# TensorE's two waits for a near down block, moved in front of the up tile that precedes the block

## The chip, the core and the metric

The kernel runs on one core of one Trainium2 chip. The metric is the device time of one execution in microseconds (us), the median of several runs. All numbers of matrices are float32; most products are made from split operands (below).

## What is computed

A block of a network for 256 tokens with 1024 features: six feed-forwards, and between them a mixer, a recurrent layer and an attention layer. The six feed-forwards are most of the work, and the only part that the change touches:

```python
def swiglu_ffn(x, w_in, w_out):                    # D_MODEL = 1024, D_FF = 2816
    gate, up = jnp.split(x @ w_in, 2, axis=-1)
    return (jax.nn.silu(gate) * up) @ w_out

x = x + 0.5 * swiglu_ffn(rms_norm(x, g), w_in, w_out)    # six times, other layers between
```

## The kernel before

**Tiles.** The hidden features of a feed-forward are cut into 22 parts (NFC) of 128, numbered c. For each part there is a *gate* tile and an *up* tile: eight steps over the 1024 input features, accumulated in one bank of PSUM. Then there is the *near* block of the part, which multiplies hid(c) by the part's rows of w_out for the first half of the outputs (four output tiles, accumulated over all c in banks 0 to 3). The second half of the outputs comes at the end, in twelve *far* blocks. Gate and up tiles use banks 4 to 7, in turn.

**Split products.** A float32 weight block w arrives by DMA in `raw`, ACT (ScalarE) rounds it into `w_hi` (L666), and POOL (GpSimd, L571) or DVE (VectorE, L1105) makes the rest `w_lo` = raw - w_hi. `three_products` makes two matmuls of a pair of weight tiles: w_hi on both halves of the moving operand (512 columns, L1866) and w_lo on the high half (256 columns, L1867). So a gate or up tile is 16 matmuls, a near block 8.

**The ring.** Weight blocks go through six slots in a written order. A slot's semaphores are `arrived`, `hi_ready`, `lo_ready` and `used`; TensorE raises `used` with the last matmul of a block, ACT waits for it before it writes the slot's w_hi again, and the load of a further block waits for `lo_ready`.

**The hidden part.** When the up tile of c is done, ACT copies the low halves out of PSUM (`take_low`, L783), DVE adds them (L1211, raises `halves_added`), multiplies by rstd (L1221), ACT takes the silu (L788), and DVE makes hid(c) in three operations (L1230, L1231, L1232; the last raises `h_ready`). Between these DVE makes the low parts of some weight blocks. Its order is written out by hand in `hidden(c)`: the low part of near block c - 1 comes first in `hidden(c)` for c > 1, so behind hid(c - 1); that of near block 0 comes inside `hidden(0)`. A near block's low part is the 128x512 form of L1105.

**TensorE's order.** In `ffn`: the tiles of c = 0 and 1, then gate_up(2), then 19 times `down(k)` and `gate_up(k + 3)` (LEAD = 3, FFN_STEPS = 19), then the near blocks 19, 20, the first far block, near block 21 and the other far blocks. `down(c)` waits for `h_ready` of c and for the `lo_ready` of its weight block. A gate tile waits for `halves_added` of part c - 2, which frees its banks, and for its `lo_ready`; an up tile waits for its `lo_ready` alone. The phases are ffn_a to ffn_f. In ffn_c DVE has also a gained copy of x to make (`gain_x`) from c = 3 on.

**Waits on TensorE.** Where an instruction has one wait, it is part of the weight load. Where it has more, the profile shows an EVENT_SEMAPHORE instruction on TensorE's sequencer with the rest of them (L1880, L1936).

Of the kernel before, what the change touches and what calls it, by code (L numbers as in the profile page):

```python
# [18 lines left out]
NFC = FF // P  # L19
# [20 lines left out]
LEAD = 3  # L40
UNUSED_PRODUCTS = 9
FFN_STEPS = NFC - LEAD
# [8 lines left out]
def gate_block(c):  # L51

    return 2 * c if c < LEAD else 2 * LEAD + 1 + 3 * (c - LEAD)


def stored_down(c):

    return 2 * LEAD + 3 * c if c < FFN_STEPS else 2 * LEAD + 3 * FFN_STEPS + c - FFN_STEPS
# [10 lines left out]
def near_block(c):  # L69

    return NEAR_LAST if c == NFC - 1 else stored_down(c)
# [141 lines left out]
def slot(n):  # L213

    return n % RING
# [20 lines left out]
def nth_split(n):  # L236

    return SPLITS_SO_FAR[n]
# [34 lines left out]
def build(nc, x_in, blocks, consts, out):  # L273
    ctx = ExitStack()
    with ctx:
# [3 lines left out]
        def sem(name):  # L279
            return ctx.enter_context(nc.semaphore(name))  # L280
# [48 lines left out]
        lo_ready = [sem(f"lo_ready{s}") for s in range(RING)]  # L329
# [24 lines left out]
        h_ready = sem("h_ready")  # L354
# [1503 lines left out]
        def _(pe):  # L1858
# [5 lines left out]
            def three_products(where, hi, lo, both, opens, closes):  # L1864

                nc.tensor.matmul(where, hi, both.rearrange("p a t -> p (a t)"), start=opens, stop=False)  # L1866
                return nc.tensor.matmul(where[:, 0:SEQ], lo, both[:, 0, :], start=False, stop=closes)  # L1867

            def feature_tiles(tiles, after_norm=None, between=None, in_halves=False):

                for k in range(KD):
                    if after_norm is not None:
                        pe.wait_ge(xn_lo_ready, KD * SPLIT_NORMS.index(after_norm) + k + 1)
                    for n, b in tiles:
                        if k == 0 and in_halves:
                            pe.wait_ge(half_lo, n + 1)
                        elif k == (KD // 2 if in_halves else 0):
                            pe.wait_ge(lo_ready[slot(n)], nth_split(n))  # L1880
                        wh, wl = (w[:, slot(n), k * P:k * P + P] for w in (w_hi, w_lo))
                        ins = three_products(ps[:, b, :], wh, wl, xn[:, k, :, :], k == 0, k == KD - 1)
                        if k == KD - 1:
                            ins.then_inc(used[slot(n)], 1)
                    if between and k == between[0]:
                        between[1]()
# [46 lines left out]
            def near_products(n0, c):  # L1933

                n = n0 + near_block(c)
                pe.wait_ge(lo_ready[slot(n)], nth_split(n))  # L1936
                for d in range(NEAR):
                    wh, wl = (w[:, slot(n), d * P:d * P + P] for w in (w_hi, w_lo))
                    ins = three_products(ps[:, d, :], wh, wl, hid[:, c, :, :], c == 0, c == NFC - 1)
                ins.then_inc(used[slot(n)], 1)  # L1940

            def far_products(n0, i):

                n, pair_no = n0 + far_block(i), i // len(GROUPS)
                group = GROUPS[i % len(GROUPS)]
                pe.wait_ge(lo_ready[slot(n)], nth_split(n))
                for d in range(2):
                    for o, c in enumerate(group):
                        at = o * PAIR + d * P
                        wh, wl = (w[:, slot(n), at:at + P] for w in (w_hi, w_lo))  # L1950
                        ins = three_products(ps[:, (4 if pair_no == 0 else 0) + d, :], wh, wl, hid[:, c, :, :], c == 0, c == NFC - 1)
                    if n == NRING - 1 and d == 0:
                        ins.then_inc(acc_done, 1)
                ins.then_inc(used[slot(n)], 1)
# [46 lines left out]
            def ffn(f, phase, total=total_squares):  # L2001
                n0 = FIRST[phase]

                def bank_of(c):
                    return 4 + 2 * (c % 2)

                def gate_up(c):
                    if c >= 2:
                        pe.wait_ge(halves_added, NFC * f + c - 1)
                    feature_tiles([(n0 + gate_block(c), bank_of(c))])  # L2010
                    feature_tiles([(n0 + gate_block(c) + 1, bank_of(c) + 1)])

                def down(c):
                    pe.wait_ge(h_ready, NFC * f + c + 1)
                    near_products(n0, c)
                norm = ("g_ffn_a", "g_ffn_b", "both", "g_ffn_d", "g_ffn_e", "g_ffn_f")[f]
                if f == 0:

                    feature_tiles([(n0, bank_of(0))], after_norm=norm, in_halves=True)
                    feature_tiles([(n0 + 1, bank_of(0) + 1)], in_halves=True)  # L2020
                    feature_tiles([(n0 + 2, bank_of(1))])
                elif norm == "both":
                    feature_tiles([(n0, bank_of(0)), (n0 + 1, bank_of(0) + 1), (n0 + 2, bank_of(1))], after_norm=norm,
                                  between=(6, total))
                elif norm == "g_ffn_e":
                    for n, b in ((n0, bank_of(0)), (n0 + 1, bank_of(0) + 1), (n0 + 2, bank_of(1))):
                        feature_tiles([(n, b)], after_norm=norm)
                    total()
                else:
                    feature_tiles([(n0, bank_of(0)), (n0 + 1, bank_of(0) + 1), (n0 + 2, bank_of(1))], after_norm=norm)  # L2030
                feature_tiles([(n0 + 3, bank_of(1) + 1)], between=None if norm in ("both", "g_ffn_e") else (1, total))
                gate_up(2)
                for k in range(FFN_STEPS):
                    down(k)
                    gate_up(k + LEAD)
                down(NFC - 3)
                down(NFC - 2)
                far_products(n0, 0)
                down(NFC - 1)
                for i in range(1, N_FAR):  # L2040
                    if i == len(GROUPS):
                        pe.wait_ge(x_ready, 4 * UPDATES_BEFORE[phase] + 1)
                    far_products(n0, i)
                pe.wait_ge(x_ready, 4 * UPDATES_BEFORE[phase] + 3)
# [421 lines left out]
            def attention():  # L2466
# [85 lines left out]
            steps = [  # L2552
                lambda: None,
                lambda: ffn(0, "ffn_a"),
                lambda: (pe.wait_ge(const_loaded, 16), mixer_one()),
                lambda: None,
                lambda: ffn(1, "ffn_b"),
                lambda: None,
                lambda: ffn(2, "ffn_c", lambda: total_squares(2, True)),
                lambda: lru(),  # L2560
                lambda: ffn(3, "ffn_d"),
# [125 lines left out]
```

## Time and profile before

| | us |
|---|---|
| median of 3 runs | 1521.01 (1520.73 to 1521.26) |
| the profiled execution | 1521.21 |
| its span, first to last instruction | 1519.4 |
| PE (TensorE matmul) busy | 1510.9 (99%) |
| DVE busy | 1052.7 (69%) |
| POOL busy | 923.4 (61%) |
| ACT busy | 776.9 (51%) |

The granted clock of TensorE was 1.0 over the span (2.4 GHz). The difference of 1.8 us between the profiled execution and its span lies before the first and behind the last instruction. Matmuls are pipelined: a row's duration is longer than the distance to the next one's start, so distances are read from start to start.

### The profile page before, as it was taken

How to read it: one execution, taken by the hardware profiler on the slowest of the kernel's cores; microseconds unless marked ns; L12 is line 12 of the kernel's file. 1: busy time of each engine (PE TensorE's matmuls, PEld its weight loads, DVE VectorE, ACT ScalarE, POOL GpSimd, SP SyncE). 2: the span in 40 equal slices, each digit the busy share in tenths (PEclk: the TensorE clock that was granted, in tenths of full speed). 3: DMA queues.
4: the chain of work that ended last, by engine and by line, in shares of the span. 5: the costliest groups of instructions: out<-in, count | busy, mean ns of one | idle time of the engine just before them, and what ended most of it. 6: DMA issues, size and time to landing. Idle time of an engine off the chain costs nothing.

```text
span 1519.4 us, 24540 instructions
## 1 busy us (share of the span) xinstructions
PE 1510.9 (99%) x9480; PEld 1315.8 (87%) x9480; DVE 1052.7 (69%) x1472; ACT 776.9 (51%) x1125; POOL 923.4 (61%) x1092
## 2 busy tenths in 40 slices
PE   9999999999999999999999999999999999999998
PEld 7888888888888888888899888888888887888887
DVE  7966555666986668976587986655466666797664
ACT  6554441123655455455567655456555456665542
POOL 4966520201687677876766687578776673168663
PEclk9999999999999999999999999999999999999999
DMA  8665633222565564665634565565555562346553
GB/s 302 209 196 183 205 99 115 85 79 86 199 212 183 168 215 160 192 205 165 228 126 167 186 210 185 183 215 187 162 189 189 186 207 94 138 156 207 188 165 119
DMA packets 113491, 263.64 MB, mean 174 GB/s; under 512 B 9184, under 2 KB 51296, under 8 KB 113248
## 3 DMA queue, kind: packets, MB, share of 16 engines
q1 hardware_dynamic: 113376, 262.09, 52.5%
q8 instruction: 75, 1.23, 0.3%
q14 instruction: 40, 0.33, 0.1%
HBM read 261.00 MB, written 1.05 MB: 172 GB/s over the span
## 4 chain that ended last, share of the span: by engine, by line
PE 74%; DVE 1%; ACT 0%; issue 0%; DVEq 0%; ACTq 0%
PE ps L1866 40%; PE ps L1867 21%; PE ps L1961 2%; PE ps L1982 2%; PE ps L1898 1%; PE ps L1899 1%; PE ps L1897 1%; PE ps L2434 1%; PE ps L2436 1%; PE ps L2435 1%; PE ps L2387 1%; PE ps L1997 0%; PE ps L1998 0%; PE ps L1996 0%; DVE arena L1812 0%; PE ps L1929 0%
## 5 line engine op out<-in xcount | busy, mean ns | idle before, releaser
L571 POOL TENSOR_TENSOR w_lo<-raw,w_hi 128x256 fp32r<-128x256 f32 x1056 | 902.4, 887 | 475.1 <-ACT w_hi L666 471.6
L1866 PE MATMUL ps<-xn,w_hi 128*128 128x512 f32 x2112 | 741.2, 393 | 0.4 <-POOL w_lo L571 0.2
L1867 PE MATMUL ps<-xn,w_lo 128*128 128x256 f32 x2112 | 591.4, 280 | 0.0
L666 ACT ACTIVATE w_hi<-raw 128x1024 fp32r<-128x1024 f32 (+1 forms) x516 | 475.5, 932 | 186.0 <-PE ps L1867 146.1
L1866 PEld LDWEIGHTS ps<-xn,w_hi 128*128 128x128 f32 x2112 | 395.1, 187 | 90.1 <-issue 0.7
L1867 PEld LDWEIGHTS ps<-xn,w_lo 128*128 128x128 f32 x2112 | 398.9, 189 | 0.2
L1866 PE MATMUL ps<-hid,w_hi 128*128 128x512 f32 x1056 | 379.4, 396 | 0.0
L1105 DVE TENSOR_TENSOR w_lo<-raw,w_hi 128x512 fp32r<-128x512 f32 (+1 forms) x245 | 284.8, 1163 | 32.5 <-ACT w_hi L666 27.6
L1867 PE MATMUL ps<-hid,w_lo 128*128 128x256 f32 x1056 | 297.1, 281 | 0.0
L1866 PEld LDWEIGHTS ps<-hid,w_hi 128*128 128x128 f32 x1056 | 198.4, 188 | 49.4
L1211 DVE TENSOR_TENSOR arena<-ps,low_part 128x512 f32<-128x512 f32 x132 | 90.8, 688 | 202.9 <-ACT low_part L783 202.9
L1867 PEld LDWEIGHTS ps<-hid,w_lo 128*128 128x128 f32 x1056 | 198.5, 188 | 0.0
L783 ACT ACTIVATE low_part<-ps 128x512 f32<-128x512 f32 x132 | 78.3, 593 | 163.8 <-PE ps L1867 163.6
L788 ACT ACTIVATE arena<-arena 128x256 f32<-128x256 f32 x132 | 55.3, 419 | 149.4 <-DVE arena L1221 149.4
L1221 DVE TENSOR_TENSOR arena<-arena,rstd 128x512 f32<-128x512 f32 x132 | 113.7, 861 | 4.5
L1913 PE MATMUL ps<-xs,raw 128*128 128x256 f32 x432 | 98.2, 382 | 0.0
L1231 DVE TENSOR_TENSOR h<-arena 128x256 f32<-128x256 f32 x132 | 91.5, 694 | 0.0
L1913 PEld LDWEIGHTS ps<-xs,raw 128*128 128x128 f32 x432 | 80.6, 190 | 12.2 <-issue 1.1
L1232 DVE TENSOR_TENSOR hid<-h,hid 128x256 fp32r<-128x256 f32 x132 | 86.0, 651 | 4.5
L1230 DVE TENSOR_TENSOR hid<-arena 128x256 fp32r<-128x256 f32 x132 | 60.7, 460 | 29.1 <-ACT arena L788 29.1
L1253 DVE SCALAR_TENSOR_TENSOR x<-ps,x 128x512 f32<-128x512 f32 x23 | 15.8, 686 | 59.6 <-PE ps L1867 59.6
L612 POOL TENSOR_TENSOR arena<-arena 128x512 f32<-128x512 f32 x4 | 4.5, 1113 | 77.5 <-DVE arena L1327 77.2
(345 smaller groups left out, 1305.8 us busy)
## 6 DMA issues: line engine op xcount, KB each, us to landing
raw<-blocks SPq DMA_DIRECT2D x418, 512.0 KB, 3.7
raw<-blocks SPq DMA_DIRECT2D x146, 256.0 KB, 3.5
cst<-consts SPq DMA_DIRECT2D x1, 2358.0 KB, 14.5
x<-x_in SPq DMA_DIRECT2D x4, 256.0 KB, 5.9
out<-x SPq DMA_DIRECT2D x4, 256.0 KB, 3.3
cst<-consts SPq DMA_DIRECT2D x1, 109.0 KB, 2.1
```

The lines of the kernel that those rows point to most:

```text
L571: ins = nc.gpsimd.tensor_tensor(w_lo[:, slot(n), piece], raw[:, slot(n), piece], w_hi[:, slot(n), piece], ALU.subtract)
L666: nc.scalar.activation(w_hi[:, slot(n), cols], raw[:, slot(n), cols], ACT.Copy)\
L783: nc.scalar.activation(low_part[:, :, :], ps[:, b:b + 2, SEQ:], ACT.Copy).then_inc(low_taken, 1)
L1105: nc.vector.tensor_tensor(w_lo[:, slot(n), cols], raw[:, slot(n), cols], w_hi[:, slot(n), cols], ALU.subtract).then_inc(lo_ready[slot(n)], 1)
L1211: nc.vector.tensor_tensor(gate_up[:, :, :], ps[:, b:b + 2, 0:SEQ], low_part[:, :, :], ALU.add)\
L1221: nc.vector.tensor_tensor(gate_up[:, :, :], gate_up[:, :, :], over(rstd[:, :], 2), ALU.mult)\
L1230: nc.vector.tensor_tensor(hid[:, c, 0, :], gate_up[:, 1, :], gs, ALU.mult)
L1231: chain(nc.vector.tensor_tensor(h[:, :], gate_up[:, 1, :], gs, ALU.mult))
L1232: nc.vector.tensor_tensor(hid[:, c, 1, :], h[:, :], hid[:, c, 0, :], ALU.subtract)\
L1866: nc.tensor.matmul(where, hi, both.rearrange("p a t -> p (a t)"), start=opens, stop=False)
L1867: return nc.tensor.matmul(where[:, 0:SEQ], lo, both[:, 0, :], start=False, stop=closes)
L1913: ins = nc.tensor.matmul(where, raw[:, slot(n), k * P:k * P + P], xs[:, k, :], start=k == 0, stop=k == KD - 1)
```

## The change

The wait for the weight block goes out of `near_products`. A new function `down_ready(c)` holds both waits of a near block. It is called between the gate tile and the up tile of gate_up(c + 2) for c = 0 to 19, and for c = 20 and 21 in `down(c)`, as before. Nothing else is changed.

```diff
@@ -1933,7 +1933,6 @@
             def near_products(n0, c):
 
                 n = n0 + near_block(c)
-                pe.wait_ge(lo_ready[slot(n)], nth_split(n))
                 for d in range(NEAR):
...
@@ -2004,14 +2003,22 @@
                 def bank_of(c):
                     return 4 + 2 * (c % 2)
 
+                def down_ready(c):
+                    n = n0 + near_block(c)
+                    pe.wait_ge(h_ready, NFC * f + c + 1)
+                    pe.wait_ge(lo_ready[slot(n)], nth_split(n))
+
                 def gate_up(c):
                     if c >= 2:
                         pe.wait_ge(halves_added, NFC * f + c - 1)
                     feature_tiles([(n0 + gate_block(c), bank_of(c))])
+                    if c >= LEAD - 1:
+                        down_ready(c + 1 - LEAD)
                     feature_tiles([(n0 + gate_block(c) + 1, bank_of(c) + 1)])
 
                 def down(c):
-                    pe.wait_ge(h_ready, NFC * f + c + 1)
+                    if c >= FFN_STEPS + 1:
+                        down_ready(c)
                     near_products(n0, c)
```

## Rows read from the trace of the kernel before

**Rows 1.** The page: engines' busy time, and the chain that ended last.

```profile
PE 1510.9 (99%) x9480; PEld 1315.8 (87%) x9480; DVE 1052.7 (69%) x1472; ACT 776.9 (51%) x1125; POOL 923.4 (61%) x1092
...
PE ps L1866 40%; PE ps L1867 21%; PE ps L1961 2%; PE ps L1982 2%; PE ps L1898 1%; PE ps L1899 1%; PE ps L1897 1%; PE ps L2434 1%; PE ps L2436 1%; PE ps L2435 1%; PE ps L2387 1%; PE ps L1997 0%; PE ps L1998 0%; PE ps L1996 0%; DVE arena L1812 0%; PE ps L1929 0%
```

**Rows 2.** Order of time, weight loads in ffn_a: an up tile's, two near blocks' (start, duration).

```profile
59.50 0.19 PEld L1866 LDWEIGHTS ps<-xn,w_hi 128*128 128x128 f32 x1
...
62.28 0.19 PEld L1866 LDWEIGHTS ps<-hid,w_hi 128*128 128x128 f32 x1
...
69.26 0.19 PEld L1866 LDWEIGHTS ps<-hid,w_hi 128*128 128x128 f32 x1
```

**Rows 3.** Order of time, VectorE: low part of the near block of 69.26.

```profile
61.67 1.11 DVE L1105 TENSOR_TENSOR w_lo<-raw,w_hi 128x512 fp32r<-128x512 f32 x1
```

**Rows 4.** Order of time, start of ffn_d: VectorE, then first loads of near blocks 0, 1.

```profile
854.88 0.43 DVE L1232 TENSOR_TENSOR hid<-h,hid 128x256 fp32r<-128x256 f32 x1
856.51 0.69 DVE L1211 TENSOR_TENSOR arena<-ps,low_part 128x512 f32<-128x512 f32 x1 [1.21 <-ACT low_part L783]
...
862.28 1.11 DVE L1105 TENSOR_TENSOR w_lo<-raw,w_hi 128x512 fp32r<-128x512 f32 x1
...
857.49 0.19 PEld L1866 LDWEIGHTS ps<-hid,w_hi 128*128 128x128 f32 x1
...
864.48 0.19 PEld L1866 LDWEIGHTS ps<-hid,w_hi 128*128 128x128 f32 x1
```

**Rows 5.** The same of near block 1 in ffn_a, b, c, e, f; block 3 of ffn_c.

```profile
31.11 1.11 DVE L1105 TENSOR_TENSOR w_lo<-raw,w_hi 128x512 fp32r<-128x512 f32 x1
...
34.33 0.19 PEld L1866 LDWEIGHTS ps<-hid,w_hi 128*128 128x128 f32 x1
...
402.86 1.11 DVE L1105 TENSOR_TENSOR w_lo<-raw,w_hi 128x512 fp32r<-128x512 f32 x1
...
406.16 0.19 PEld L1866 LDWEIGHTS ps<-hid,w_hi 128*128 128x128 f32 x1
...
590.08 1.11 DVE L1105 TENSOR_TENSOR w_lo<-raw,w_hi 128x512 fp32r<-128x512 f32 x1
...
592.30 0.19 PEld L1866 LDWEIGHTS ps<-hid,w_hi 128*128 128x128 f32 x1
...
1087.60 1.11 DVE L1105 TENSOR_TENSOR w_lo<-raw,w_hi 128x512 fp32r<-128x512 f32 x1
...
1095.49 0.19 PEld L1866 LDWEIGHTS ps<-hid,w_hi 128*128 128x128 f32 x1
...
1351.92 1.11 DVE L1105 TENSOR_TENSOR w_lo<-raw,w_hi 128x512 fp32r<-128x512 f32 x1
...
1354.52 0.19 PEld L1866 LDWEIGHTS ps<-hid,w_hi 128*128 128x128 f32 x1
...
603.35 0.72 DVE L1105 TENSOR_TENSOR w_lo<-raw,w_hi 128x512 fp32r<-128x512 f32 x1
...
606.27 0.19 PEld L1866 LDWEIGHTS ps<-hid,w_hi 128*128 128x128 f32 x1
```

**Rows 6.** Order of time, ffn_a: GpSimd's last piece, and the weight load it released.

```profile
20.98 0.73 POOL L571 TENSOR_TENSOR w_lo<-raw,w_hi 128x256 fp32r<-128x256 f32 x1
...
21.82 0.19 PEld L1866 LDWEIGHTS ps<-xn,w_hi 128*128 128x128 f32 x1 [0.52 <-issue]
```

**Rows 7.** Order of time, matmuls: pairs 3, 4 of ffn_d's block 0; pair 3 of ffn_a's block 20.

```profile
858.31 0.42 PE L1866 MATMUL ps<-hid,w_hi 128*128 128x512 f32 x1
...
858.69 0.39 PE L1866 MATMUL ps<-hid,w_hi 128*128 128x512 f32 x1
...
162.35 0.39 PE L1866 MATMUL ps<-hid,w_hi 128*128 128x512 f32 x1
```

**Rows 8.** TensorE's event instructions: before a near block in ffn_a; before gate tiles in ffn_d.

```profile
L1936 PEldq EVENT_SEMAPHORE  x1: 51/51/51, 66.3 to 66.3; - x1
...
L1880 PEldq EVENT_SEMAPHORE  x2: 51/51/51, 858.6 to 863.6; - x2
```

## The prediction, made before the changed kernel was run

> **What bounds the kernel now.** First the page: TensorE (PE) is busy 1510.9 us of the span and its two lines L1866 and L1867 carry the chain that ended last [rows 1]. So only what PE does, or what makes PE wait, can move the end, and any time in which PE stands still is added in full unless PE has idle time further on that swallows it; it has 8.5 us of such time in the whole kernel. The question is therefore where TensorE would arrive at the moved waits before their semaphores are there.
>
> The second view is the order of time inside a feed-forward. In the steady state the up tile starts at 59.50, the near block behind it at 62.28, the next near block at 69.26 [rows 2]: an up tile takes 2.78 us (16 matmuls in pairs of 0.347 us) and one iteration 6.98 us. The moved waits therefore ask for their semaphores 2.78 us earlier than now. Nothing stands still in these iterations: the 114 distances from one near block to the next are all 6.96 to 6.99 us, of which rows 2 show one.
>
> **The change, part by part.** In each of the six feed-forwards, 20 near blocks (c = 0 to 19) lose both waits at their start, and the same two waits come before the up tile of gate_up(c + 2). The blocks 20 and 21 keep theirs where they were. No matmul, weight load, DMA or semaphore is added or taken away: 120 pairs of waits move past 16 matmuls each. Queued behind them on PE are the up tile, the near block and the next gate tile; who waits for these is ACT (low_part of the up tile), DVE behind it, and the ring (ACT's splitting into w_hi and the loads on SP's queue wait for the slots). They are all late by the same amount as PE, no more. No other queue is passed.
>
> *Late iterations: nothing.* Once VectorE has caught up, the last of the two semaphores is the one of the near block's low parts. For the near block at 69.26 it comes at 61.67 + 1.11 = 62.78 [rows 3], and the up tile in front starts at 69.26 - 2.78 = 66.48: 3.7 us to spare, against 6.5 us now, and more later, as VectorE goes on to catch up. The wait costs nothing there; what hides it is VectorE's lead of a whole iteration.
>
> *First iterations: TensorE stands still.* At the start of a feed-forward VectorE has no lead: it has just made rstd. In the fourth one (ffn_d) h(0) is there at 854.88 + 0.43 = 855.31; near block 0 starts at 857.49, in time [rows 4], but its up tile starts at 857.49 - 2.78 = 854.71: 0.60 us late. Worse is the next one. The low half of near block 1 is made by VectorE behind h(1), at 862.28 + 1.11 = 863.39, and near block 1 starts at 864.48; its up tile starts at 864.48 - 2.78 = 861.70, so TensorE would wait 1.69 us [rows 4]. The same subtraction for the others [rows 5], low half of near block 1 against the start of near block 1 less 2.78:
> ffn_a 32.22 - 31.55 = 0.67; ffn_b 403.97 - 403.38 = 0.59; ffn_c 591.19 - 589.52 = 1.67; ffn_f 1353.03 - 1351.74 = 1.29; ffn_e 1088.71 against 1092.71, 4.0 us to spare. Sum with ffn_d: 5.91 us.
>
> The stall at up tile 2 (h(0), 0.60 us in ffn_d, and about as much or less in the other four, where the same steps of VectorE stand in the same place) is not added to that, if what makes block 1 late isn't driven by TensorE: the late moment is then fixed, and the first stall only brings TensorE there later. I take that, since between h(0) and the low half of block 1 VectorE waits only once, 1.21 us for ACT's low_part of tiles finished before [rows 4], and works without a gap otherwise. Behind block 1 the shift of 0.6 to 1.7 us is itself the margin for the following blocks: the tightest is ffn_c, where the gained copy of x holds VectorE up. Its near block 3 is at 606.27 with its low half at 603.35 + 0.72 = 604.07 [rows 5], 0.58 us late for an up tile at 603.49 on today's clock, which is less than the 1.67 us that TensorE is behind by then.
>
> *Restart.* A wait that is served adds the time from semaphore to weight load. A gate tile in ffn_a that waited for its low part shows it: GpSimd ends at 20.98 + 0.73 = 21.71, the weight load starts at 21.82 [rows 6], 0.11 us. Five stalls: 0.55 us. Two stalls in place of one don't double it, because the first is inside the second's time.
>
> *The waits themselves.* Three waits stand now before an up tile (h_ready, the near block's, its own), of which one rides on the weight load and the rest on an event instruction. Such an event costs 51 ns on TensorE's sequencer, which ran 2.9 us ahead: the one for the near block at 69.26 is at 66.3 [rows 2, 8]. I take zero for it; the bound upward is one event more per iteration in full, 114 x 0.051 = 5.8 us, and nothing speaks for it, since the events of today lie under 1.44 us or more of queued matmuls. The Trainium skill (Perfetto Trace Analysis, Sequencer-only Instruction) says that the sequencer itself sits in the semaphore wait of such an instruction and that its record begins when all are satisfied. By that rule the event of the moved waits is asked for near 3 us before the up tile, and blocks only the filling of the queue; the trace agrees, since an event held the sequencer until 858.6 [rows 8] while the near block of 857.49 ran on.
>
> *What the near block loses.* The near blocks are not perfect today: the third pair of a near block takes 858.69 - 858.31 = 0.38 us, where pairs take 0.35, and its first matmul 0.42 us instead of 0.39 [rows 7]. It looks like a price of the waits, and 117 of the 120 near blocks that lose them have it (counted in the order of time; rows 7 show one), some 1.44 us for four pairs against 1.39 at an up tile's pace. I don't credit the change with it. First, near block 20 of ffn_a has the same two waits and follows another near block; the first matmul of its third pair, at 162.35, takes 0.39 us [rows 7]. Second, the extra time comes two pairs behind the wait. Third, at 858.31 the sequencer was held at the next event until 858.6 [rows 8], so it isn't the sequencer's work either. Taken all the same, the gain is 117 x 0.05 = 5.9 us at most, and 117 x 0.035 = 4.1 us if the block then runs as block 20.
>
> The Trainium skill (TensorE: Matmul & The Clock Gate, Step-by-step: what each phase is for) has weight loads pulled ahead of running matmuls, which a wait on the weight load would prevent; by it the near block should gain. The near block's first weight load already starts at 857.49, with the last matmul of the up tile, as every other weight load does, so this trace leaves it nothing to pull.
>
> **Sum.** 5.91 + 0.55 = +6.5 us on the profiled execution of 1521.21 (span 1519.4 to 1525.9), 1527.7. The median of the runs, 1521.01, is 0.2 lower: 1527.5.
>
> **Rivals.**
> A. *The near block's extra 0.04 to 0.05 us comes from the waits after all* and goes with them. Stalls +6.5, gain -4.1 to -5.9: 1521.6 to 1523.4, no change that a measurement of this kernel can tell (about 0.2%, 3.0 us). For it: the place, every near block behind an up tile. Against: block 20. It decides the sign of the verdict when a near block gains more than (6.5 - 3.0)/117 = 0.030 us. Chance 0.12.
> B. *The stalls add up.* If VectorE's chain is driven by TensorE after all, then each late block costs its own deficit: beside the 6.5 us, five first stalls of up to 0.60 us with a restart each (3.5 us) and late blocks in ffn_c of 0.58 us each, three at most (2.0 us): up to 1533.0, about 1531.5 if the first stalls of the others are half as long. Against: the gapless VectorE rows. Chance 0.09.
> C. *The change beats before.* For this the near block must gain all 0.05 us and VectorE must reach block 1 earlier, for instance since a standing TensorE disturbs the other engines less; with half the stalls, 3.2 us, and 5.9 us gained the time is 1518.3. Only the first half of it has anything in the trace. Chance 0.03.
> D. *Something new at the up tile.* Its first pairs get the 0.05 us that the near block has today, which then keeps its own: 120 x 0.05 = 6 us more, 1533.5. Against: block 20 runs at its normal pace right behind two waits [rows 7]. Chance 0.04.
> E. *No stall*, the waits being satisfied earlier than I read: 1521.0. The rows' subtraction leaves no room for it. Chance 0.02.
> The forecast has 0.70.
>
> **Numbers.** The forecast's own range is 1526.9 (the stalls of 5.9 us, restarts hidden) to 1529.0 (half of the first stalls added). To leave out no more than 2 in 10 the range takes in B, and A's upper edge: 1523.0 to 1531.5. Slower by over 0.2%: forecast, B, D and a sixth of A, 0.85. Within 0.2%: the rest of A, and E, 0.12. Faster: C, 0.03.
>
> **What the profile of the changed kernel would show.** At the up tiles 2 and 3 of five feed-forwards an idle weight-load row, released by VectorE: in ffn_d 0.6 us and then 1.1 to 1.2 us (1.69 + 0.11 less the first), in ffn_c the same, in ffn_a and ffn_b 0.6 and then 0.1 to 0.2, in ffn_f less at first and 1.4 in all; none in ffn_e. From near block 4 on an iteration should still be 6.98 us, with the third near pair at 0.38 us. If it is 6.94 us, A is right. If up tiles 4 to 9 of ffn_c show idle time, B is. I am wrong as well if the first stall delays h(1): then block 1's low half comes later than 863.4 on the shifted clock of ffn_d.

## The result, and the profile after

The changed kernel takes 1527.38 us (median of 5 runs, 1527.13 to 1527.55), the kernel before 1521.01 in the same comparison: a ratio of 1.0042, 95% interval 1.0027 to 1.0057. The forecast was 1527.5, 6.5 us slower; measured were 6.4 us.

The page of the changed kernel (span, busy times, then the chain that ended last):

```profile
span 1525.5 us, 24540 instructions
PE 1511.6 (99%) x9480; PEld 1314.9 (86%) x9480; DVE 1042.1 (68%) x1472; ACT 779.2 (51%) x1125; POOL 914.1 (60%) x1092
...
PE 72%; DVE 4%; issue 0%; ACT 0%; DVEq 0%; ACTq 0%
```

PE has the same 9480 matmuls and nearly the same busy time as in rows 1, in a span that is 6.1 us longer: TensorE hardly works longer (0.7 us), it stands: 8.5 us without a matmul before, 13.9 us now. DVE now has 4% of the chain (1% before), because where TensorE waits the chain goes back into VectorE's work.

The order of time shows where. These are all weight loads from up tile 2 of a feed-forward to near block 19 that the view gives idle time in brackets (with it, where the profile could tell, who ended it); in turn two of ffn_a, one of ffn_b, two each of ffn_c, ffn_d and ffn_f:

```profile
24.92 0.19 PEld L1866 LDWEIGHTS ps<-xn,w_hi 128*128 128x128 f32 x1 [0.58 <-DVE hid L1232]
32.03 0.19 PEld L1866 LDWEIGHTS ps<-xn,w_hi 128*128 128x128 f32 x1 [0.19 <-issue]
...
397.50 0.19 PEld L1866 LDWEIGHTS ps<-xn,w_hi 128*128 128x128 f32 x1 [0.71 <-DVE hid L1232]
...
584.38 0.19 PEld L1866 LDWEIGHTS ps<-xn,w_hi 128*128 128x128 f32 x1 [0.63 <-DVE hid L1232]
592.49 0.19 PEld L1866 LDWEIGHTS ps<-xn,w_hi 128*128 128x128 f32 x1 [1.15 <-issue]
...
858.35 0.19 PEld L1866 LDWEIGHTS ps<-xn,w_hi 128*128 128x128 f32 x1 [0.70 <-DVE hid L1232]
866.45 0.19 PEld L1866 LDWEIGHTS ps<-xn,w_hi 128*128 128x128 f32 x1 [1.14 <-issue]
...
1349.72 0.19 PEld L1866 LDWEIGHTS ps<-xn,w_hi 128*128 128x128 f32 x1 [0.27 <-DVE hid L1232]
1357.82 0.19 PEld L1866 LDWEIGHTS ps<-xn,w_hi 128*128 128x128 f32 x1 [1.15 <-issue]
```

The first tiles of ffn_a have idle loads in front of these, in the kernel before too, and they aren't the change's. 0.04 us of each is the ordinary distance between two weight loads. The second load of ffn_b waited 0.10 us and is too short for a bracket; ffn_e has none. "Issue" doesn't say who was late, because that wait sits in an event instruction and not in the load itself. VectorE's rows beside it do. In ffn_d of the changed kernel, h(0), h(1) and the low half of near block 1 (start, duration):

```profile
857.87 0.43 DVE L1232 TENSOR_TENSOR hid<-h,hid 128x256 fp32r<-128x256 f32 x1
859.50 0.69 DVE L1211 TENSOR_TENSOR arena<-ps,low_part 128x512 f32<-128x512 f32 x1 [1.20 <-ACT low_part L783]
...
864.40 0.85 DVE L1232 TENSOR_TENSOR hid<-h,hid 128x256 fp32r<-128x256 f32 x1
865.28 1.10 DVE L1105 TENSOR_TENSOR w_lo<-raw,w_hi 128x512 fp32r<-128x512 f32 x1
```

h(0) ends at 857.87 + 0.43 = 858.30 and the load of up tile 2 starts at 858.35; the low half ends at 866.38 and the load of up tile 3 starts at 866.45. From h(0)'s start to the low half's end VectorE took 8.51 us, the same as before, 863.39 - 854.88 [rows 4]: the standing TensorE didn't delay it. From h(0)'s end to the low half's end the same holds in the other four: the two kernels differ by 0.02 us at most.

### The profile page after: what moved, and what is told of

It reads as the page before. It is cut to its first block, busy times and chain, and to the rows that moved or that the text cites. A ratio compares the mean times of both kernels' runs of the same rounds, so it can differ in the third digit from the quotient of the medians.

```text
span 1525.5 us, 24540 instructions
## 1 busy us (share of the span) xinstructions
PE 1511.6 (99%) x9480; PEld 1314.9 (86%) x9480; DVE 1042.1 (68%) x1472; ACT 779.2 (51%) x1125; POOL 914.1 (60%) x1092
## 4 chain that ended last, share of the span: by engine, by line
PE 72%; DVE 4%; issue 0%; ACT 0%; DVEq 0%; ACTq 0%
PE ps L1866 38%; PE ps L1867 20%; PE ps L1960 2%; PE ps L1981 2%; PE ps L1897 1%; PE ps L1899 1%; PE ps L1898 1%; PE ps L2441 1%; PE ps L2443 1%; PE ps L2442 1%; PE ps L2394 1%; DVE w_lo L1105 0%; PE ps L1997 0%; PE ps L1996 0%; PE ps L1995 0%; DVE arena L1812 0%
## 5 line engine op out<-in xcount | busy, mean ns | idle before, releaser
L571 POOL TENSOR_TENSOR w_lo<-raw,w_hi 128x256 fp32r<-128x256 f32 x1056 | 892.9, 879 | 489.6 <-ACT w_hi L666 486.0
L1105 DVE TENSOR_TENSOR w_lo<-raw,w_hi 128x512 fp32r<-128x512 f32 (+1 forms) x245 | 281.0, 1148 | 32.0 <-ACT w_hi L666 27.1
```

The lines of the kernel that those rows point to most:

```text
L571: ins = nc.gpsimd.tensor_tensor(w_lo[:, slot(n), piece], raw[:, slot(n), piece], w_hi[:, slot(n), piece], ALU.subtract)
L1105: nc.vector.tensor_tensor(w_lo[:, slot(n), cols], raw[:, slot(n), cols], w_hi[:, slot(n), cols], ALU.subtract).then_inc(lo_ready[slot(n)], 1)
```

## The experiments

All times are medians; each ratio is to the kernel before in the same comparison.

**1. All but the first two near blocks.** The waits of near blocks 0 and 1 stay where they were.

```diff
-                    if c >= LEAD - 1:
+                    if c >= LEAD + 1:
                         down_ready(c + 1 - LEAD)
...
-                    if c >= FFN_STEPS + 1:
+                    if c < 2 or c >= FFN_STEPS + 1:
                         down_ready(c)
```

> The waits of near blocks 2 to 19 are moved in front of the up tile, those of blocks 0 and 1 stay where they were. Late-start theory (VectorE has no lead at the start of a feed-forward, and only up tiles 2 and 3 wait): as before, 1521.0, within 0.5 us, and no idle weight load in the iterations. Rival, a price of the three waits at each up tile: 18 of 20 parts of the loss stay, about 1526.7. Rival, late blocks 3, 4 and 6 of ffn_c on the unshifted clock: if TensorE isn't already behind, block 3 alone costs 0.58 + 0.11 us, so 1521.7; this one is possible together with the first theory, since here nothing delays TensorE before block 3.

Measured: 1521.64, ratio 1.0005 (0.9996 to 1.0014). Eighteen of twenty pairs of waits are moved. The 0.66 us between the medians are not clear of the noise, but the order of time shows a stall and its place, which the last rival of the expectation had named: block 3 of ffn_c (the load of its up tile):

```profile
604.06 0.19 PEld L1866 LDWEIGHTS ps<-xn,w_hi 128*128 128x128 f32 x1 [0.64 <-issue]
```

The late-start theory by itself, with no idle load anywhere, missed this one. A price for each up tile is excluded. In the changed kernel this stall isn't there: TensorE is 1.7 us behind by then, as the prediction had it. So block 3 is late by itself, and hidden by the earlier stall.

**2. The first two near blocks alone.** `if LEAD - 1 <= c <= LEAD` in gate_up, `if c >= 2` in down.

> Only the waits of near blocks 0 and 1 of each feed-forward are moved. Late-start theory: the whole loss, 1527.4. Price of the waits at each up tile: 2 of 20 parts, 1521.6.

Measured: 1527.34, ratio 1.0042 (1.0030 to 1.0055), the whole loss with 12 of the 120 pairs of waits.

**3. The low part's wait alone.** h_ready goes back to the near block.

```diff
                 def down_ready(c):
                     n = n0 + near_block(c)
-                    pe.wait_ge(h_ready, NFC * f + c + 1)
                     pe.wait_ge(lo_ready[slot(n)], nth_split(n))
...
                 def down(c):
+                    pe.wait_ge(h_ready, NFC * f + c + 1)
```

> Only the wait for the near block's low part is moved, h_ready stays at the near block. Late-start theory, with the first stall (at up tile 2, by h_ready) lying inside the second (at up tile 3, by the low part): the whole loss, 1527.4, with no stall at up tile 2 and 0.7, 0.7, 1.8, 1.8, 1.4 us at up tile 3 of ffn_a, b, c, d, f. Rival, the two stalls add up: the loss is smaller by the first stalls, some 2.6 us, 1524.8.

Measured: 1527.38, ratio 1.0044 (1.0031 to 1.0058), the same as with both. The order of time has one stall for each feed-forward, at up tile 3; its rows for ffn_c, d and f:

```profile
592.21 0.19 PEld L1866 LDWEIGHTS ps<-xn,w_hi 128*128 128x128 f32 x1 [1.74 <-DVE w_lo L1105]
...
866.11 0.19 PEld L1866 LDWEIGHTS ps<-xn,w_hi 128*128 128x128 f32 x1 [1.80 <-DVE w_lo L1105]
...
1357.49 0.19 PEld L1866 LDWEIGHTS ps<-xn,w_hi 128*128 128x128 f32 x1 [1.36 <-DVE w_lo L1105]
```

In ffn_d 1.80 stands in the place of 0.70 + 1.14 with both waits. The first stall lies inside the second, and now the releaser is named, since the wait rides on the load.

**4. h_ready alone.** The low part's wait goes back to the near block.

> Only the wait for h_ready is moved, that for the near block's low part stays at the near block. Late-start theory: per feed-forward the larger of what h(0) and h(1) are late on the clock of before, plus 0.04 us of restart: 0.60, 0.56, 0.59, 0.64 and 0.24 us in ffn_a, b, c, d, f, in all 2.6 us, 1523.6. If the stalls add up, 4.0 us, 1525.0.

Measured: 1523.89, ratio 1.0020 (1.0011 to 1.0029): +2.9 us. The order of time has the five stalls at up tile 2 (0.55, 0.66, 0.59, 0.66 and 0.23 us, 2.7 in all) and none at up tile 3. With experiment 3: 6.4 and 2.9 us apart, 6.4 together.

**5 and 6. One more operation on VectorE**, before h(1) is finished, in the changed kernel and in the kernel before:

```diff
                     chain(nc.vector.tensor_tensor(h[:, :], gate_up[:, 1, :], gs, ALU.mult))
+                    if c == 1:
+                        chain(nc.vector.tensor_tensor(h[:, :], gate_up[:, 1, :], gs, ALU.mult))
```

> The changed kernel, in which VectorE makes h(1) of each feed-forward twice (one more 128x256 multiply of 0.41 to 0.96 us, as L1231 takes at that place, in the chain that ends in the low part of near block 1). If VectorE's chain alone sets when TensorE goes on, each of the five stalls at up tile 3 grows by that operation: 0.4 to 1.0 us each, 2 to 5 us in all, about 1531; ffn_e, with 4.0 us to spare, stays free. If something else sets it (ACT's rounding, the arrival of the weights, the event instruction), nothing is added, 1527.4.

> The same additional operation in the kernel before. There near block 1 itself waits, 2.78 us later, with 1.09 us to spare in ffn_d and 1.11 in ffn_c by the clock of before: the operation of up to 0.96 us fits, 1521.0, with at most 0.1 us of waiting. If an operation on VectorE costs time for another reason than the moved wait, it shows here too, and the result of the changed kernel with it isn't to be read as the wait's.

Measured: 1531.69 in the changed kernel (ratio 1.0070, 1.0058 to 1.0083), 1521.26 in the one before (1.0002, 0.9993 to 1.0011). The new operation and the load of up tile 3 in ffn_d of the changed kernel with it:

```profile
866.75 0.84 DVE L1233 TENSOR_TENSOR h<-arena 128x256 f32<-128x256 f32 x1
...
869.66 0.19 PEld L1868 LDWEIGHTS ps<-xn,w_hi 128*128 128x128 f32 x1 [2.01 <-issue]
```

The operation of 0.84 us makes the stall 0.87 us longer (2.01 against 1.14). In the other four feed-forwards it grows by 0.86 to 0.89 us, and between the medians of the two kernels lie 4.3 us. The same operation costs nothing before: block 1, which waits 2.78 us later, has the room. VectorE's chain sets when TensorE goes on.

**7. The near block's banks in reverse order**, in the kernel before (`for d in reversed(range(NEAR))`).

> The kernel before with the four output tiles of each near block in the reverse order (PSUM banks 3, 2, 1, 0). The near block's third pair takes 0.38 us instead of 0.35. If that belongs to the position behind the up tile, the third pair (now bank 1) is the long one; if it belongs to bank 2, the second pair is. 1521.0 in both cases.

Measured: 1521.1 in its one run. The third pair is still the long one, now in bank 1, so it belongs to the position and not to bank 2 (order of time, pairs 3 and 4 of a near block of ffn_a):

```profile
63.03 0.42 PE L1866 MATMUL ps<-hid,w_hi 128*128 128x512 f32 x1
...
63.42 0.39 PE L1866 MATMUL ps<-hid,w_hi 128*128 128x512 f32 x1
```

**8. Near blocks on xn in place of hid**, waits as before (the first half of each feed-forward's output is another product).

```diff
-                    ins = three_products(ps[:, d, :], wh, wl, hid[:, c, :, :], c == 0, c == NFC - 1)
+                    ins = three_products(ps[:, d, :], wh, wl, xn[:, c % KD, :, :], c == 0, c == NFC - 1)
```

> The kernel before, in which the near blocks multiply xn in place of hid, with the same waits (so the first half of each feed-forward's output is another product). If the near block's extra 0.05 us comes from reading hid behind xn, all 20 pairs of an iteration take 0.347 us, an iteration 6.93 us, and the time is about 1515. If it comes from the PSUM banks, the position or the waits, an iteration stays at 6.98 us and the time at 1521.0.

Measured: 1519.91, but from 1517.14 to 1523.13 in 10 runs; ratio 0.9990 (0.9981 to 0.9999). In ffn_a of the profiled execution the long pair is gone (order of time, a near block's second to fourth pair), an iteration is 6.93 us:

```profile
62.12 0.39 PE L1866 MATMUL ps<-xn,w_hi 128*128 128x512 f32 x1
...
62.47 0.39 PE L1866 MATMUL ps<-xn,w_hi 128*128 128x512 f32 x1
...
62.82 0.39 PE L1866 MATMUL ps<-xn,w_hi 128*128 128x512 f32 x1
```

So the extra 0.05 us of a near block comes with the moving operand hid. The time fell by only 1.1 us in place of 6, with a spread that no other kernel had shown till then; the last experiment shows what lies behind it.

**9 to 11. hid at another address.** A free tensor of 32 bytes in each partition (64 in the tenth) in front of the arena that holds hid. It moves hid and whatever else lies in the arena (gate_up and gs of the hidden part, which ACT and DVE use) by as much, so the experiment speaks for the arena's address, and for hid's own only with experiment 8 beside it. Before the shift, hid begins 32 bytes past a multiple of 64, xn at a multiple of 64. The eleventh is the changed kernel with the 32 bytes.

```diff
+        sb("pad", [P, 8])
         arena_at = nc.sbuf_base
```

> The kernel before, with 32 bytes of each partition left free in front of the arena that holds hid. hid then begins at a multiple of 64 bytes (of 512 even), as xn does; before it begins 32 bytes past one. If the extra time of matmuls on hid comes from this, every pair of matmuls on hid takes 0.347 us: an iteration 6.93 us in place of 6.99 (117 x 0.053 us), and the far blocks 0.0033 us less for each of 600 pairs: about -6 and -2 us, 1513. If it comes from hid being written by VectorE shortly before, or from anything else in hid, 1521.0.

> The control: 64 bytes left free, so that hid moves too but is again 32 bytes past a multiple of 64. 1521.0 and iterations of 6.99 us if the alignment is the cause; about 1513 if any shift of the arena will do.

> The changed kernel with the 32 bytes of the aligned one. The stalls at up tiles 2 and 3 are set by VectorE and don't depend on it: 6.4 us slower than the aligned kernel before, about 1519.5, if alignment gives 8 us. Up to 0.1 us per feed-forward may go either way, since near block 0, which stands between the two stalls, gets faster.

Measured: 1528.91 (1.0054, 1.0041 to 1.0066), 1527.01 (1.0041, 1.0027 to 1.0055) and 1534.76 (1.0092, 1.0076 to 1.0107). My theory of the alignment fell: both shifts make the kernel slower. The long pair is gone indeed, a near block takes 1.40 us; but the gate and up tiles, at 0.347 us for a pair before, now take 0.353. Stretches of 110 us in ffn_b, the kernel before and then the one with the 32 bytes (columns: stretch, its length, busy time and instructions of each engine, clock, DMA share, GB/s):

```profile
410.00:520.00 110.00, 110.00 (x631) 96.52 (x630) 80.44 (x106) 56.31 (x80) 85.75 (x100) 1.00 0.60 196
```

```profile
410.00:520.00 110.00, 110.00 (x625) 95.61 (x625) 78.94 (x105) 55.00 (x79) 83.55 (x99) 1.00 0.57 189
```

TensorE is busy for all of both, at a clock of 1.00, and ends 631 matmuls in one and 625 in the other. An iteration is 7.05 us in place of 6.99. The eleventh is 5.9 us slower than the ninth, so the stalls of the moved waits come on top of it unchanged.

**12. hid and xn at the same place within 2048 bytes.** The free tensor has 1696 bytes.

> The kernel before with 1696 bytes of each partition left free in front of the arena, so that hid begins 128 bytes past a multiple of 2048, as xn does (each part of hid and of xn is 2048 bytes). The near blocks on xn ran without any extra time, the two shifts of 32 and 64 bytes made all gate and up tiles slower. If the pace of the matmul pairs follows from where the two moving operands lie to each other within 2048 bytes, all pairs take 0.347 us, an iteration 6.93 us, and the time is about 1513. If any shift of the arena brings the slow pace of 0.353 us, about 1527 to 1529. If neither, the pace isn't settled by this address and stays open.

Measured: a median of 1523.00, in 12 runs from 1515.92 to 1529.77; ratio 1.0017 (0.9998 to 1.0036). The profiled execution shows both paces in one kernel. Four stretches, in ffn_a, ffn_b, ffn_d and ffn_e:

```profile
40.00:150.00 110.00, 110.00 (x625) 95.41 (x624) 77.20 (x104) 56.37 (x80) 82.56 (x98) 1.00 0.59 193
410.00:520.00 110.00, 110.00 (x636) 96.19 (x636) 83.09 (x107) 56.59 (x82) 87.60 (x101) 1.00 0.59 193
...
870.00:980.00 110.00, 110.00 (x636) 97.00 (x636) 82.43 (x109) 57.46 (x83) 83.13 (x97) 1.00 0.60 195
1100.00:1210.00 110.00, 110.00 (x625) 95.31 (x624) 69.90 (x101) 55.74 (x79) 76.21 (x95) 1.00 0.57 184
```

Whole feed-forwards run at 0.347 us for a pair (636 matmuls, 6.93 us an iteration, near blocks without extra time) and whole ones at 0.353 (625, 7.07 us). In all six a feed-forward keeps the pace that up tile 2 had. Experiment 8 shows the same: 637 or 636 matmuls in five feed-forwards, 625 in ffn_e. One feed-forward at the slow pace costs about 3 us by my estimate (19 iterations of 0.13 us, and 0.0067 us for each of 100 pairs behind them). That the spread between runs comes from how many begin at the fast pace fits this, but isn't shown: one execution of each kernel is traced. No version here beats the kernel before reliably.

## Why the prediction was right

*The first iterations.* The largest term, and right. What each feed-forward added, read as the shift of near block 19 against the kernel before, stands beside the term plus 0.11 us of restart:

| | ffn_a | ffn_b | ffn_c | ffn_d | ffn_e | ffn_f | sum |
|---|---|---|---|---|---|---|---|
| predicted, us | 0.78 | 0.70 | 1.78 | 1.80 | 0 | 1.40 | 6.46 |
| measured, us | 0.48 | 0.75 | 1.75 | 1.77 | 0.00 | 1.30 | 6.05 |

Experiments 1 and 2 show the place, 5 and 6 that VectorE's chain is the cause. ffn_a is 0.3 us short. The idle times there, 0.54 and 0.15 us, are close to the forecast's; the rest is that this execution came to up tile 2 earlier than the kernel before (the load in front of it at 24.14 against 24.36 us). Experiments 2 and 3 had 0.71 and 0.25 us in ffn_a by the same reading, so this one figure varies from one execution to the next. That the medians agree with the sum to 0.1 us (1527.38 and 1527.5), where the trace has 0.4 us less, is in part luck.

*Inside, not added.* Right: experiments 3, 4 and the changed kernel (6.4, 2.9 and 6.4 us) fit one fixed moment for each feed-forward: the prices of the two waits moved apart make 9.3 us, moved together 6.4. Rival B (1531.5) is excluded. The tightest block behind, block 3 of ffn_c, was free in the changed kernel and cost 0.64 us as soon as TensorE came in time (experiment 1).

*Restart.* 0.11 us was somewhat large. In all five feed-forwards 0.07 us lie between the low half and the load of up tile 3; 0.05 us where h_ready ended the wait, and in experiment 3, where the low half's wait rides on the load itself. Five times 0.04 us is 0.2 us of the 0.4 that the sum was too high.

*The waits themselves and the late iterations.* Zero, as taken: in experiment 1, where 108 pairs of waits are moved, the iterations outside the start of ffn_c are 6.99 us or less, but for 0.04 us before one up tile of ffn_d. Rival D is out.

*The near block's extra time.* The step that I weighed longest. It was rightly not credited. In the changed kernel these 120 near blocks have no wait at all, and 110 keep it (order of time, pairs 3 and 4 in ffn_a):

```profile
63.57 0.42 PE L1866 MATMUL ps<-hid,w_hi 128*128 128x512 f32 x1
...
63.96 0.39 PE L1866 MATMUL ps<-hid,w_hi 128*128 128x512 f32 x1
```

0.39 us for the pair as in rows 7, so rivals A and C are out. The ten without it are all blocks 0 and 1, and come in at another pace than the rest (below). The Trainium skill (TensorE: Matmul & The Clock Gate, Step-by-step: what each phase is for) has weight loads pulled ahead of running matmuls. As a reason for a gain here it is out: with the waits gone, the first weight load of near blocks 2 to 19 starts 0.11 us ahead of its matmul, as before. What I gave for the cause, "not the waits", is shown; I had no cause to offer, and the experiments give only a part of one (below).

## What to carry to other kernels

When a wait moves ahead on the bounding engine, its price is made at the few places where the producer has no lead yet, the starts of stages; the steady state says nothing of them, so subtract there, stage by stage. A stall that ends at a moment which the waiting engine doesn't influence hides the earlier ones and the smaller late ones behind it: take the largest for a stage, not their sum. It hides them only while it lasts: with it gone (experiment 1), the next one shows. And a small regular excess at the place of a wait isn't the wait's until a row without the wait lacks it.

## What was not expected of the hardware

A stream of the same pairs of weight loads and matmuls (512 and 256 columns) runs at either of two steady paces, 0.347 or 0.353 us for a pair (here the two products of one weight block), with TensorE busy and its clock at 1.00 in both. The long third pair of a near block (0.38 to 0.39 us) could be taken for the sign of a return to the fast pace. The traces say otherwise. In ffn_b of the changed kernel, up tile 3 runs at the slow pace behind its stall: three pairs from 405.40 to 406.46 take 1.06 us. Near block 1, from 407.52, has no long pair (its third runs from 408.23 to 408.57), takes 1.41 us in place of 1.44, and the gate tile behind it runs at the fast pace all the same: three pairs from 409.28 to 410.32 take 1.04 us.

```profile
405.40 0.40 PE L1866 MATMUL ps<-xn,w_hi 128*128 128x512 f32 x1
...
406.46 0.40 PE L1866 MATMUL ps<-xn,w_hi 128*128 128x512 f32 x1
...
407.52 0.40 PE L1866 MATMUL ps<-hid,w_hi 128*128 128x512 f32 x1
...
408.23 0.39 PE L1866 MATMUL ps<-hid,w_hi 128*128 128x512 f32 x1
...
408.57 0.39 PE L1866 MATMUL ps<-hid,w_hi 128*128 128x512 f32 x1
...
408.93 0.40 PE L1866 MATMUL ps<-xn,w_hi 128*128 128x512 f32 x1
409.28 0.39 PE L1866 MATMUL ps<-xn,w_hi 128*128 128x512 f32 x1
...
410.32 0.39 PE L1866 MATMUL ps<-xn,w_hi 128*128 128x512 f32 x1
```

Counted over near blocks 0 to 19 of the kernel before and the changed one: the 227 that a tile of even pairs of 0.347 us precedes have the long pair; the 13 behind a tile at 0.353 us, or with pairs of 0.350 and 0.343 us in turn, have none. So the long pair is what a near block costs that comes in at the even fast pace, and a return to that pace doesn't need it.

What a near block does to the pace of the tiles behind it depends on its moving operand (experiment 8) and on the arena's address (9 to 12). With hid at its first place, they run at 0.347 us whatever came in (until a stall, behind which the slow pace can start anew, as in up tile 3 above). With the arena moved by 32 or 64 bytes they run at 0.353 us, also where block 0 came in at 0.347 (four feed-forwards each), and an iteration takes 7.05 us in place of 6.99. Where the near blocks read xn (experiment 8), or hid at the same place as xn within 2048 bytes (experiment 12), the pace stays as it came in. ffn_e shows it best: up tile 2 takes 0.353 us for a pair in the kernel before and in experiment 8; the first goes on at the fast pace behind near block 0, the second stays slow. A stretch of ffn_e in the kernel before and in experiment 8:

```profile
1100.00:1210.00 110.00, 110.00 (x631) 96.50 (x631) 70.88 (x103) 56.08 (x79) 77.37 (x96) 1.00 0.59 187
```

```profile
1100.00:1210.00 110.00, 110.00 (x625) 95.36 (x624) 70.78 (x103) 54.85 (x79) 74.23 (x92) 1.00 0.57 184
```

So the long pair looked like a loss of 6 us in all, but every kernel whose near blocks were all free of it was slower by 6 us or more, or ran at both paces. Why the operand and its address act like this, what sets the pace at the start of a stage, and how a kernel could keep the fast one throughout (6.93 us an iteration, about 1513 to 1515 us by the estimates of experiments 8 and 12), stays open.
